# Rings of the split weight tiles four deep instead of two, each tile split by one 1024-column instruction, and a software DMA scratch of 2048 bytes

## The chip, the cores and the metric

The kernel runs on one core of one Trainium2 chip. The metric is the device time of one launch, in microseconds. The engines named below are PE (TensorE, matmuls; PEld is its weight load), ACT (ScalarE), DVE (VectorE), POOL (GpSimd, which here only issues DMAs from the software queue) and SP (SyncE, which issues the DMAs of the hardware queue).

## What is computed

A two-layer trunk on x of 256 tokens by 1024. Each layer has an attention mixer and then a channel mixer with retrieved experts (PEER). The change touches only the second part, which the reference writes so:

```python
def peer(h, w_q, sub_keys, u_tab, v_tab):
    q = jnp.einsum('td,de->te', xt, w_q).reshape(t, PEER_HEADS, 2, PEER_DQ // 2)
    sc = jnp.einsum('thpd,hpnd->thpn', q, sub_keys)          # 8 heads, 2 sides, 128 keys
    # top 16 of each side, top 16 of their 256 sums: eidx (one of 128*128 experts), gates
    ...
    a = jnp.einsum('tkd,td->tk', u_tab[ib], xb)              # u row of each picked expert
    a = jax.nn.gelu(a, approximate=False) * gb
    return jnp.einsum('tk,tkd->td', a, v_tab[ib])            # weighted sum of v rows
for l in range(DEPTH):                                       # DEPTH = 2
    x = x + g1 * mixer(...)
    x = x + g2 * peer(rmsnorm(x, norm_ffn[l]) * (1 + sc2) + sh2, ...)
```

The kernel does not gather. It computes the scores of all 16,384 experts for all tokens (128 tiles of 128 experts), applies a dense table of gates that is zero where an expert was not picked, and multiplies with all of v.

## The kernel before, in words

**Tiles and numbers.** A tile of u or v is 128 partitions by 1024 columns of float32 (512 KB). PE multiplies in one-pass float32r, so each tile is split in two parts: ACT copies it to `hi` (rounded), DVE computes `lo = raw - hi`. Three products (hi with x_hi, hi with x_lo, lo with x_hi) stand for one float32 product.

**The stages of a layer's expert part** (`experts` of each engine):
- *Queries and retrieval*: PE makes the queries and key scores; DVE finds the top 16s, partly beside the first u tiles.
- *Up*: for each of 128 u tiles, PE runs 24 matmuls of 256 columns (`up`), ACT applies gelu to the result (`gelu`), and SP spills it to `s_store` in HBM. Between them stand the matmuls that transpose the picks (`picks`) and build the gate table (`group`).
- *Down*: for each of 128 v tiles, SP fetches the spilled scores into one of four buffers (`back`), DVE multiplies them by the gates (`weigh`), ACT and DVE split the product into a_hi and a_lo (`split_a`, `lower_a`, rings of two), and PE runs 12 matmuls of 512 columns (`down`).

**The rings.** `raw` holds four tiles as loaded. `hi` and `lo` hold two tiles (`SPLITS`), filled and released by halves: `split(n, r, h, ...)` on ACT and `lower(n, r, h)` on DVE work on 512 columns, and the semaphores hi_done, lo_done and w_used count halves.

**What sets the order.** Everything is written out by hand, with one program for each engine, each in strict order. In the down stage, step j is:
- ACT (`down_step`): both halves of split for tile j+2, then `split_a` for tile j+2, which waits until PE has finished tile j.
- DVE (`down_step`): `weigh` for j+2, both halves of lower for j+2, `lower_a` for j+2. In layer 0, every fourth step then reduces one tile of layer 1's modulation weights (`next_modulation`).
- SP (`down_loads`): load v tile j once `lo` of tile j-4 is done, then fetch the scores of tile j+1, which waits for `lower_a` of tile j-3 (al_done). In layer 0, after every fourth tile (j % 4 == 2), it also issues a load of 512 KB of modulation weights (`load_mod1`), ahead of v tile j+1.
- POOL, in layer 0's down stage: seven loads of layer 1's w_in and bias tables into parts of the gate table that are no longer needed, each as soon as `weigh` has come far enough.

In the up stage, step n of ACT is: the first half of split n+2, gelu n, the second half of split n+2. PE's `up(n)` waits for gelu n-2, since two PSUM banks alternate.

Of the kernel before, what the change touches and what calls it, by code (L numbers as in the profile page):

```python
# [8 lines left out]
ALU = mybir.AluOpType  # L9
ACT = mybir.ActivationFunctionType  # L10
F32 = mybir.dt.float32
# [4 lines left out]
P = 128  # L16
# [17 lines left out]
SPLITS = 2  # L34
# [102 lines left out]
def build(nc, a, out):  # L137

    with ExitStack() as ctx:
# [178 lines left out]
        def _(sp):  # L318
# [16 lines left out]
            for l in range(LAYERS):  # L335
# [33 lines left out]
                for n in range(4, 8):  # L369
                    sp.wait_ge(s[l]["lo_done"], 2 * n - 6)  # L370
                    load_u(n, n % 4)
                    if n >= 6:
                        spill(n - 6, n - 6)
                with sp.Fori(2, NKEY // 4) as i:
                    for r in range(4):
                        sp.wait_ge(s[l]["lo_done"], 8 * i + 2 * r - 6)
# [8 lines left out]
                for n in range(NKEY, NKEY + 8):  # L385
                    sp.wait_ge(s[l]["lo_done"], 2 * n - 6)
# [6 lines left out]
                def down_loads(j, i, r, fetches=True):  # L393
                    sp.wait_ge(s[l]["lo_done"], STREAM - 6 + 2 * j)
# [22 lines left out]
                sp.wait_ge(s[l]["lo_done"], 2 * STREAM)  # L417
# [40 lines left out]
        def _(pe):  # L458
# [178 lines left out]
            def experts(l):  # L637

                def up(n, r, wait=True):
# [3 lines left out]
                    o = bank[4 + r][:, 0:T]  # L643
                    for h in range(2):
                        pe.wait_ge(s[l]["hi_done"], 2 * n + h + 1)
                        pe.wait_ge(s[l]["lo_done"], 2 * n + h + 1)
                        for k in range(h * KT // 2, (h + 1) * KT // 2):
                            c = slice(k * P, (k + 1) * P)
                            mm(o, hi[:, r, c], x_hi[:, k, :], k == 0, False)
                            mm(o, hi[:, r, c], x_lo[:, k, :], False, False)  # L650
                            last = mm(o, lo[:, r, c], x_hi[:, k, :], False, k == KT - 1)
                        last.then_inc(s[l]["w_used"], 1)
# [10 lines left out]
                def down(j, r, first=False, end=False):  # L663

                    pe.wait_ge(s[l]["ah_done"], j + 1)
                    pe.wait_ge(s[l]["al_done"], j + 1)
                    for h in range(2):
                        pe.wait_ge(s[l]["hi_done"], STREAM + 2 * j + h + 1)
                        pe.wait_ge(s[l]["lo_done"], STREAM + 2 * j + h + 1)
                        c = slice(h * HALF, (h + 1) * HALF)  # L670
                        for t in range(TT):
                            o, tok = bank[2 * t + h][:, :], slice(t * P, (t + 1) * P)
                            mm(o, a_hi[:, r, tok], hi[:, r, c], first, False, True)
                            mm(o, a_hi[:, r, tok], lo[:, r, c], False, False, True)
                            last = mm(o, a_lo[:, r, tok], hi[:, r, c], False, end, True)
                        last.then_inc(s[l]["w_used"], 1)
# [3 lines left out]
                up(0, 0, False)  # L680
                up(1, 1, False)
# [752 lines left out]
```

## Time and profile before

| | us |
|---|---|
| median of 3 runs (lowest, highest) | 2186.24 (2186.05, 2189.31) |
| the profiled execution, its own time | 2186.42 |
| its span | 2184.6 |
| PE busy, share of the span | 94% |
| PEld | 84% |
| DVE | 67% |
| ACT | 47% |
| DMA queues, hardware / software, share of 16 engines | 57.6% / 6.2% |

The span is the time from the first to the last instruction in the profile; the execution's own time is 1.8 us longer. Busy times are sums over an engine's instructions, and as matmuls are pipelined and their ends modelled, a busy PE is not one at its peak: the distance from one matmul's start to the next tells more. The down stage of layer 0 lies at 764.2 to 1139.4 us, that of layer 1 at 1818.75 to 2167.3 us.

### The profile page before, as it was taken

To read this page: it belongs to the slowest core of one execution; us is meant where nothing else is said; L and a number is where in the kernel's file an instruction comes from. 1 tells how busy PE (TensorE), PEld (TensorE's weight loads), DVE (VectorE), ACT (ScalarE), POOL (GpSimd) and SP (SyncE) were. 2 spreads that over 40 slices of the span, in tenths; PEclk is the share of its full clock that TensorE was granted. 3 is DMA by queue.
4 is the path that set the end of the run, shared out by engine and by line. 5 is a ranking of instruction groups with operands and counts; after the bars stand their busy time and mean duration, and the time that the engine had idled before them with its cause. 6 is when DMAs were issued, how large, how long until landed. Compare 5 with 4: busy or idle time off the path is not lost.

```text
span 2184.6 us, 43826 instructions
## 1 busy us (share of the span) xinstructions
PE 2064.4 (94%) x12608; PEld 1839.8 (84%) x12608; DVE 1463.0 (67%) x3698; ACT 1022.4 (47%) x2012; POOL 18.8 (1%) x39
## 2 busy tenths in 40 slices
PE   2987899999999999999999799999999999999998
PEld 2745799999999977777778478999999998888886
DVE  4463687837777577788771327784877756777776
ACT  2012235635555555555551322563555555555554
POOL 0000000000000000000000000000000000000000
PEclk5998899999999999999999899999999999999999
DMA  9653537736566789998860412774555568777774
GB/s 396 236 187 141 199 111 229 219 108 177 172 176 171 240 292 308 309 318 280 310 216 1 173 41 85 236 221 125 173 176 172 176 194 250 242 241 241 241 241 157
DMA packets 168453, 446.75 MB, mean 204 GB/s; under 512 B 18752, under 2 KB 85568, under 8 KB 163792
## 3 DMA queue, kind: packets, MB, share of 16 engines
q1 hardware_dynamic: 163472, 392.65, 57.6%
q0 software_dynamic: 4928, 53.45, 6.2%
q8 instruction: 27, 0.44, 0.1%
q14 instruction: 26, 0.21, 0.0%
HBM read 409.32 MB, written 36.70 MB: 204 GB/s over the span
## 4 chain that ended last, share of the span: by engine, by line
PE 88%; DMA 5%; DVE 3%; ACT 2%; issue 1%; SPq 0%; DVEq 0%; ACTq 0%
PE bank L460 87%; DMA raw<-in_v 3%; DMA big<-in_w_mod 2%; DMA wmod_ring<-in_w_mod 1%; ACT big L787 1%; DVE big L954 1%; DVE big L1011 1%; PE bank L532 1%; DVE wmod_ring L1320 0%; ACT hi L834 0%; SPq L330 0%; DVE raw L946 0%; DVE a_lo L1194 0%; PE bank L710 0%; DVE big L1043 0%
## 5 line engine op out<-in xcount | busy, mean ns | idle before, releaser
L1175 DVE TENSOR_TENSOR lo<-raw,hi 128x512 fp32r<-128x512 f32 x1024 | 702.9, 691 | 377.8 <-ACT hi L834 372.1
L834 ACT ACTIVATE hi<-raw 128x512 fp32r<-128x512 f32 x1024 | 642.1, 629 | 515.1 <-PE bank L460 477.3
L460 PE MATMUL bank<-x_hi,hi 128*128 128x256 f32 x2048 | 590.2, 288 | 1.6 <-ACT work L840 1.6
L460 PE MATMUL bank<-x_hi,lo 128*128 128x256 f32 x2048 | 579.2, 283 | 0.0
L460 PE MATMUL bank<-x_lo,hi 128*128 128x256 f32 x2048 | 579.1, 283 | 0.0
L460 PE MATMUL bank<-hi,a_hi 128*128 128x512 f32 x1024 | 403.0, 394 | 13.8 <-DVE a_lo L1194 12.4
L460 PE MATMUL bank<-hi,a_lo 128*128 128x512 f32 x1024 | 400.1, 391 | 0.0
L460 PE MATMUL bank<-lo,a_hi 128*128 128x512 f32 x1024 | 399.8, 390 | 0.0
L460 PEld LDWEIGHTS bank<-x_hi,hi 128*128 128x128 f32 x2048 | 392.3, 192 | 1.9 <-issue 1.9
L460 PEld LDWEIGHTS bank<-x_lo,hi 128*128 128x128 f32 x2048 | 392.7, 192 | 0.0
L460 PEld LDWEIGHTS bank<-x_hi,lo 128*128 128x128 f32 x2048 | 392.1, 191 | 0.0
L460 PE MATMUL bank<-raw,big 128*128 128x256 f32 (+1 forms) x1248 | 287.3, 390 | 30.6 <-ACT raw L761 29.1
L460 PEld LDWEIGHTS bank<-raw,big 128*128 128x128 f32 (+1 forms) x1248 | 238.2, 193 | 70.4 <-issue 35.3
L460 PEld LDWEIGHTS bank<-hi,a_hi 128*128 128x128 f32 x1024 | 192.8, 188 | 66.6 <-issue 26.3
L460 PEld LDWEIGHTS bank<-hi,a_lo 128*128 128x128 f32 x1024 | 193.0, 188 | 40.9
L460 PEld LDWEIGHTS bank<-lo,a_hi 128*128 128x128 f32 x1024 | 193.0, 189 | 39.3
L840 ACT ACTIVATE work<-bank 128x256 f32<-128x256 f32 x256 | 98.3, 384 | 195.6 <-PE bank L460 194.9
L1183 DVE TENSOR_SCALAR wmod_ring<-cst,wmod_ring 128x128 f32<-128x128 f32 x512 | 142.4, 342 | 0.0
L460 PE MATMUL bank<-wmod_ring 128*128 128x128 f32 x1024 | 135.1, 275 | 0.0
L460 PEld LDWEIGHTS bank<-wmod_ring 128*128 128x128 f32 x1024 | 125.7, 192 | 0.0
L1189 DVE TENSOR_TENSOR wmod_ring<-wmod_ring,big 128x256 f32<-128x256 f32 x256 | 107.2, 420 | 0.8 <-DMA wmod_ring<-s_store 0.8
L862 ACT ACTIVATE a_hi<-wmod_ring 128x256 fp32r<-128x256 f32 x256 | 103.5, 404 | 8.4 <-DVE wmod_ring L1189 8.3
(142 smaller groups left out, 1313.2 us busy)
## 6 DMA issues: line engine op xcount, KB each, us to landing
raw<-in_u SPq DMA_DIRECT2D x256, 512.0 KB, 4.0
raw<-in_v SPq DMA_DIRECT2D x256, 512.0 KB, 4.5
s_store<-work SPq DMA_DIRECT2D x256, 128.0 KB, 3.7
wmod_ring<-s_store SPq DMA_DIRECT2D x256, 128.0 KB, 3.5
wmod_ring<-in_w_mod SPq DMA_DIRECT2D x54, 512.0 KB, 5.4
big<-in_w_mod SPq DMA_DIRECT2D x40, 512.0 KB, 5.1
big<-in_w_in POOLq DMA_DIRECT2D x10, 2048.0 KB, 11.6
big<-in_w_q POOLq DMA_DIRECT2D x16, 1024.0 KB, 6.5
```

The lines of the kernel that those rows point to most:

```text
L460: return nc.tensor.matmul(o, w, x, start=start, stop=stop, skip_group_check=free)
L532: last = nc.tensor.transpose(bank[4 + n % 2][:, c * P:(c + 1) * P], scores[:, i, c * P:(c + 1) * P], ident)
L787: last = f(c, c, ACT.Exp, bias=neg[:, 2 * i + t:2 * i + t + 1], accum_out=den[:, 2 * i + t:2 * i + t + 1])
L834: f(hi[:, r % 2, c], raw[:, r, c], ACT.Copy).then_inc(s[l]["hi_done"], 1)
L840: f(work[:, r, :], bank[4 + r % 2][:, 0:T], ACT.Gelu).then_inc(s[l]["s_gelu"], 1)
L862: f(a_hi[:, r % 2, :], back[:, b, :], ACT.Copy).then_inc(s[l]["ah_done"], 1)
L954: v.tensor_tensor_reduce(first_mods[r], first_mods[r], c_all[:], 1.0, 0.0, ALU.mult, ALU.add, mod[l][:, n:n + 1]).then_inc(s[l]["mod_tile" ...
L1011: v.tensor_tensor_reduce(scores[:, i, c], bank[i % 4][:, c], b[:, c], 1.0, -3e38, ALU.add, ALU.max, mx[:, 2 * i + t:2 * i + t + 1]).then_i ...
L1175: v.tensor_tensor(lo[:, r % 2, c], raw[:, r, c], hi[:, r % 2, c].bitcast(F32), ALU.subtract).then_inc(s[l]["lo_done"], 1)
L1183: ins = v.tensor_scalar(hot[r % 2][:, 1, n, :], iota, pick[:, 1, bass.ds(4 * g + n, 1)], pick[:, 2, bass.ds(4 * g + n, 1)], ALU.is_equal, ...
L1189: v.tensor_tensor(back[:, b, :], back[:, b, :], gates[:, bass.ds(j, 1), :].rearrange("p a t -> p (a t)"), ALU.mult)\
```

## The change

`SPLITS` is 4, so `hi` and `lo` together take 16 KB more of each partition, and the scratch that is set aside for the descriptors of software DMAs goes from its default down to 2048 bytes of a partition. Split and lower become one instruction of 1024 columns each, and hi_done, lo_done and w_used count tiles. Split of tile n now waits for w_used of tile n-4 and stands one tile further ahead in ACT's and DVE's programs: the up step n does split n+3 and then gelu n; the down step j does split (and lower) for j+3, and then `split_a` (and `lower_a`) for j+2. PE's loops are unrolled by four instead of two, and `up` and `down` wait once for a tile instead of once for a half. What SP issues, in which order, and what each issue waits for is the same but for the counting.

```diff
-SPLITS = 2
+SPLITS = 4
@@ SP
                 def down_loads(j, i, r, fetches=True):
-                    sp.wait_ge(s[l]["lo_done"], STREAM - 6 + 2 * j)
+                    sp.wait_ge(s[l]["lo_done"], NKEY - 3 + j)
                     load_v(j, r)
                     if fetches:
                         fetch(j + 1, (r + 1) % 4, i + (1 if r == 3 else 0))
@@ PE
-                    for h in range(2):
-                        pe.wait_ge(s[l]["hi_done"], 2 * n + h + 1)
-                        pe.wait_ge(s[l]["lo_done"], 2 * n + h + 1)
-                        for k in range(h * KT // 2, (h + 1) * KT // 2):
...
+                    pe.wait_ge(s[l]["hi_done"], n + 1)
+                    pe.wait_ge(s[l]["lo_done"], n + 1)
+                    for k in range(KT):
...
+                    last.then_inc(s[l]["w_used"], 1)
@@ ACT
-                def split(n, r, h, round_, wait=True):
+                def split(n, r, round_, wait=True):
                     act.wait_ge(raw_in[r], 16 * (round_ + 1) + 16 * l * (STREAM // RAWS))
                     if wait:
-                        act.wait_ge(s[l]["w_used"], 2 * n + h - 3)
-                    c = slice(h * HALF, (h + 1) * HALF)
-                    f(hi[:, r % 2, c], raw[:, r, c], ACT.Copy).then_inc(s[l]["hi_done"], 1)
+                        act.wait_ge(s[l]["w_used"], n - 3)
+                    f(hi[:, r], raw[:, r], ACT.Copy).then_inc(s[l]["hi_done"], 1)
...
                 def up_step(n, r, round_, wait=True):
-                    nr, nround = (r + 2) % 4, round_ + (r + 2) // 4
-                    split(n + 2, nr, 0, nround)
+                    split(n + 3, (r + 3) % 4, round_ + (r + 3) // 4, wait or r > 0)
                     gelu(n, r, round_, wait)
-                    split(n + 2, nr, 1, nround)
...
                 copy_keys(PH - 1)
+                split(2, 2, 0, False)
...
-                def down_step(j, r, round_):
-                    nr, nround = (r + 2) % 4, round_ + (r + 2) // 4 + NKEY // 4
-                    for h in range(2):
-                        split(NKEY + 2 + j, nr, h, nround)
-                    split_a(j + 2, r, nr)
+                def down_step(j, a, r, round_):
+                    if j is not None:
+                        split(NKEY + 3 + j, (r + 3) % 4, round_ + (r + 3) // 4 + NKEY // 4)
+                    split_a(a, r, (r + 2) % 4)
@@ DVE
-                def lower(n, r, h):
-                    dve.wait_ge(s[l]["hi_done"], 2 * n + h + 1)
-                    c = slice(h * HALF, (h + 1) * HALF)
-                    v.tensor_tensor(lo[:, r % 2, c], raw[:, r, c], hi[:, r % 2, c].bitcast(F32), ALU.subtract).then_inc(s[l]["lo_done"], 1)
+                def lower(n, r):
+                    dve.wait_ge(s[l]["hi_done"], n + 1)
+                    v.tensor_tensor(lo[:, r], raw[:, r], hi[:, r].bitcast(F32), ALU.subtract).then_inc(s[l]["lo_done"], 1)
...
+                def down_step(j, r, round_, mods=None, left=True):
                     weigh(j + 2, (r + 2) % 4, round_ + (r + 2) // 4)
-                    for half in range(2):
-                        lower(NKEY + 2 + j, (r + 2) % 4, half)
+                    if left:
+                        lower(NKEY + 3 + j, (r + 3) % 4)
                     lower_a(j + 2, r, (r + 2) % 4)
                     if mods:
                         next_modulation(*mods)
@@ host
-    nc = bacc.Bacc("TRN2", target_bir_lowering=False, num_devices=1)
+    nc = bacc.Bacc("TRN2", target_bir_lowering=False, num_devices=1, dynamic_dma_scratch_size=2048)
```

ACT, layer 0's down loop, its first step (j a multiple of four), before. `raw_in2` is the load of tile j+2, w_used_0 the count of what PE has used.

```order
L832 ISA [waits raw_in2]
L834 ACTIVATE hi<-raw 128x512 [waits w_used_0]
L832 REGISTER_ALU [waits raw_in2]
L834 ACTIVATE hi<-raw 128x512 [waits w_used_0]
L859 REGISTER_ALU
L861 ISA [waits a_ready_0]
L862 ACTIVATE a_hi<-wmod_ring 128x256 [waits w_used_0]
```

The same step in the changed kernel.

```order
L834 ISA [waits raw_in3]
L835 ACTIVATE hi<-raw 128x1024 [waits w_used_0]
L858 REGISTER_ALU
L860 REGISTER_ALU [waits a_ready_0]
L861 ACTIVATE a_hi<-wmod_ring 128x256 [waits w_used_0]
```

The split ahead of `a_hi` of tile j+2 is now that of tile j+3, whose load is raw_in3.

DVE, the same step before; s_in2 is the fetch of the scores of tile j+2.

```order
L1189 ISA [waits s_in2]
L1189 TENSOR_TENSOR wmod_ring<-wmod_ring,big 128x256
L1173 ISA
L1175 TENSOR_TENSOR lo<-raw,hi 128x512 [waits hi_done_0]
L1173 REGISTER_ALU
L1175 TENSOR_TENSOR lo<-raw,hi 128x512 [waits hi_done_0]
L1193 REGISTER_ALU
L1194 TENSOR_TENSOR a_lo<-wmod_ring,a_hi 128x256 [waits ah_done_0]
```

And in the changed kernel.

```order
L1186 ISA [waits s_in2]
L1186 TENSOR_TENSOR wmod_ring<-wmod_ring,big 128x256
L1171 REGISTER_ALU
L1172 TENSOR_TENSOR lo<-raw,hi 128x1024 [waits hi_done_0]
L1190 REGISTER_ALU
L1191 TENSOR_TENSOR a_lo<-wmod_ring,a_hi 128x256 [waits ah_done_0]
```

One instruction of 1024 columns, for tile j+3, stands where two of 512 for tile j+2 stood; `a_lo` behind it is still that of tile j+2.

ACT, layer 0, where the up stage begins, before: the copies of `hi` are of tile 2 and then of tile 3, and `work` is gelu of tile 0.

```order
L834 ACTIVATE hi<-raw 128x512 [waits w_used_0,raw_in2]
L840 ACT_TABLE_LOAD
L840 ACTIVATE work<-bank 128x256 [waits w_used_0]
L834 ACTIVATE hi<-raw 128x512 [waits w_used_0,raw_in2]
L834 ACTIVATE hi<-raw 128x512 [waits w_used_0,raw_in3]
```

And in the changed kernel.

```order
L835 ACTIVATE hi<-raw 128x1024 [waits raw_in2]
L835 ACTIVATE hi<-raw 128x1024 [waits raw_in3]
L841 ACT_TABLE_LOAD
L841 ACTIVATE work<-bank 128x256 [waits w_used_0]
```

Two whole tiles are split ahead of the first gelu, where half of one was.

## Rows read from the trace of the kernel before

**Rows 1.** Stretches of both down stages: us; busy by engine; PEclk, DMA share, GB/s.

```profile
764.20:1139.40 375.20, 361.18 (x1538) 287.58 (x1536) 295.44 (x607) 201.65 (x382) 3.71 (x7) 0.99 0.88 296
1818.75:2167.30 348.55, 348.35 (x1538) 288.11 (x1536) 260.06 (x508) 199.54 (x382) 0.00 (x0) 1.00 0.76 237
```

**Rows 2.** Waits of PE in layer 0's down stage: us, times, longest.

```profile
PE bank L460 <- DVE a_lo L1194: 12.4, 6, 3.6
```

**Rows 3.** Chain of waits: start us, us, what; first and last of a kind.

```profile
778.03 11.16 PE bank L460 x48
...
1108.54 11.17 PE bank L460 x48
```

**Rows 4.** Timeline of layer 0's down stage around one modulation load: start us, us.

```profile
828.11 0.39 PE L460 MATMUL bank<-hi,a_hi 128*128 128x512 f32 x1
828.31 0.63 ACT L834 ACTIVATE hi<-raw 128x512 fp32r<-128x512 f32 x1 [0.73 <-PE bank L460]
828.85 0.40 ACT L862 ACTIVATE a_hi<-wmod_ring 128x256 fp32r<-128x256 f32 x1
...
829.58 0.42 DVE L1194 TENSOR_TENSOR a_lo<-wmod_ring,a_hi 128x256 fp32r<-128x256 f32 x1
...
830.18 0.33 SPq L350 DMA_DIRECT2D wmod_ring<-s_store  x1
...
830.78 0.33 SPq L333 DMA_DIRECT2D wmod_ring<-in_w_mod  x1
...
831.41 0.33 SPq L340 DMA_DIRECT2D raw<-in_v  x1
...
832.64 1.22 DVE L1199 CUSTOM_DVE_ANT_0 wmod_ring<-wmod_ring,c_all 128x1024 f32<-128x1024 f32 x1
...
835.69 0.42 DVE L1194 TENSOR_TENSOR a_lo<-wmod_ring,a_hi 128x256 fp32r<-128x256 f32 x1
...
836.47 0.47 PE L460 MATMUL bank<-hi,a_hi 128*128 128x512 f32 x1
...
838.25 0.63 ACT L834 ACTIVATE hi<-raw 128x512 fp32r<-128x512 f32 x1 [0.84 <-DMA raw<-in_v]
```

**Rows 5.** Landing of raw's loads at 864:898, 975:1037, 1830:2160, 480:740, in order.

```profile
DMA to landing us min/median/max: 4.2/4.7/6.2
DMA to landing us min/median/max: 3.9/5.0/6.7
DMA to landing us min/median/max: 3.5/4.3/5.2
DMA to landing us min/median/max: 3.7/3.8/4.2
```

**Rows 6.** Chain of waits through v loads issued beside POOL's loads.

```profile
802.91 11.00 DMA raw<-in_v
...
816.35 0.34 issue
...
1038.54 12.59 DMA raw<-in_v
```

**Rows 7.** Busy time by stretch, just after PE's stall at 861.9 to 863.9.

```profile
863.90:867.30 3.40, 3.40 (x8) 2.66 (x9) 1.90 (x4) 2.07 (x4) 0.00 (x0) 0.53 1.03 375
```

**Rows 8.** Groups by form: busy us, mean ns, idle before.

```profile
L1175 DVE TENSOR_TENSOR lo<-raw,hi 128x512 fp32r<-128x512 f32 x1024 | 702.9, 691 | 377.8 <-ACT hi L834 372.1
L1325 DVE TENSOR_TENSOR x_lo<-raw,x_hi 128x2048 fp32r<-128x2048 f32 x2 | 4.6, 2293 | 5.1 <-ACT x_hi L827 5.1
L822 ACT ACTIVATE big<-raw 128x1024 f32<-128x1024 f32 x1 | 1.1, 1057 | 1.5 <-DVE raw L1051 1.5
```

**Rows 9.** Timeline where layer 0's up stage begins.

```profile
309.55 0.36 PE L460 MATMUL bank<-x_hi,hi 128*128 128x256 f32 x1
311.74 0.63 ACT L834 ACTIVATE hi<-raw 128x512 fp32r<-128x512 f32 x1 [1.32 <-DMA raw<-in_u]
312.39 1.28 ACT L840 ACT_TABLE_LOAD   x1
```

More of the change, by code:

```diff
@@ L672, in down @@
                             o, tok = bank[2 * t + h][:, :], slice(t * P, (t + 1) * P)
[L673 to L676, printed above, removed]
+                            mm(o, a_hi[:, r % 2, tok], hi[:, r, c], first, False, True)
+                            mm(o, a_hi[:, r % 2, tok], lo[:, r, c], False, False, True)
+                            last = mm(o, a_lo[:, r % 2, tok], hi[:, r, c], False, end, True)
+                    last.then_inc(s[l]["w_used"], 1)
                 pe.wait_ge(s[l]["xh_done"], 1)
                 pe.wait_ge(s[l]["xl_done"], 1)
-                up(0, 0, False)
-                up(1, 1, False)
-                with pe.Fori(1, GROUP_AT // 2 - 1) as i:
-                    for r in range(2):
-                        up(2 * i + r, r)
+                for r in range(4):
+                    up(r, r, r >= 2)
+                with pe.Fori(1, GROUP_AT // 4 - 1) as i:
+                    for r in range(4):
+                        up(4 * i + r, r)
+                for r in range(2):
+                    up(GROUP_AT - 4 + r, r)
                 picks(l)
-                for r in range(2):
-                    up(GROUP_AT - 2 + r, r)
+                for r in range(2, 4):
+                    up(GROUP_AT - 4 + r, r)
                 for r in range(4):
-                    up(GROUP_AT + r, r % 2)
+                    up(GROUP_AT + r, r)
                     group(r, r, False)
@@ L692, in experts @@
                     for r in range(4):
[L693 removed]
+                        up(GROUP_AT + 4 * i + r, r)
                         group(4 * i + r, r)
[L695 to L697 removed]
+                with pe.Fori((GROUP_AT + GROUPS) // 4, NKEY // 4) as i:
+                    for r in range(4):
+                        up(4 * i + r, r)
                 pe.wait_ge(s[l]["g_copied"], GROUPS)
                 down(0, 0, first=True)
[L700 to L703 removed]
+                with pe.Fori(0, NKEY // 4 - 1) as i:
+                    for r in range(4):
+                        down(4 * i + 1 + r, (1 + r) % 4)
+                for r in range(1, 4):
+                    down(NKEY - 4 + r, r, end=r == 3)
             def expert_out(l):
@@ L1219, in experts @@
                         for n in range(2):
-                            for half in range(2):
-                                lower(n, n, half)
+                            lower(n, n)
                 for n in range(GROUP_AT - 2):
-                    for half in range(2):
-                        lower(n + 2, (n + 2) % 4, half)
-                        advance(500)
+                    lower(n + 2, (n + 2) % 4)
+                    advance(1000)
                 for _ in left:
@@ L1232, in experts @@
                 for g in range(4):
-                    for half in range(2):
-                        lower(GROUP_AT + g, g, half)
+                    lower(GROUP_AT + g, g)
                     one_hot(g, g, g >= 2)
@@ L1237, in experts @@
                     for r in range(4):
-                        for half in range(2):
-                            lower(GROUP_AT + 4 * i + r, r, half)
+                        lower(GROUP_AT + 4 * i + r, r)
                         one_hot(4 * i + r, r)
@@ L1242, in experts @@
                     for r in range(4):
-                        for half in range(2):
-                            lower(4 * i + r, r, half)
+                        lower(4 * i + r, r)
                 dve.wait_ge(s[l]["g_copied"], GROUPS)
```

55 lines of the change are left out of this document (22 added, 33 removed).

## The prediction

> **What bounds the kernel now.** I read the busy time by stretch first. Layer 1's down stage shows a clean PE: 128 tiles in 348.55 us, 2.72 us a tile, PE busy all the time [rows 1]. Layer 0's, with the same 128 tiles, takes 375.20 us, 26.65 us more [rows 1]. The list of PE's waits and the starts of its matmuls in both layers' up stages show next to nothing, so these 26.65 us are nearly all that a deeper ring could give back, and they are the place where it can also lose. Three things fill them.
>
> First, PE's chain runs there in pieces of 48 matmuls, four tiles, of 11.16 or 11.17 us [rows 3], against 4 x 2.72 = 10.89. Each piece ends in a gap of about 0.28 us; I count 27 such gaps among the starts, from 778.03 to 1119.74 us: 27 x 0.28 = 7.6 us. The timeline around one of them shows why. DVE spends 1.22 us on the modulation weights at 832.64; a_lo of the next tile then starts at 835.69 and ends at 836.11, and PE starts at 836.47 instead of at about 836.27 [rows 4]. Second, PE waits for a_lo six times, 12.4 us in all, up to 3.6 [rows 2]. Here v loads landed late: the load issued at 802.91 took 11.00 us, the one at 1038.54 took 12.59 [rows 6], because a software DMA of 2 or 3 MB ran at that moment (POOL issues seven such loads there, five of them large). Third, the clock: after the stall that ended at 863.90 the granted clock was 0.53 for 3.4 us, 1.2 instead of 2.4 GHz, and eight matmuls ran in the time of four [rows 7], 1.6 us lost. After one other stall it was the same. 7.6 + 12.4 + 3.2 leaves 3.4 us for restarts and a slightly slower pace.
>
> **The time line of a v tile.** All of the rest hangs on this. Call the tile Y and count from the moment t = 0 at which PE starts tile Y-5 (828.11 in the rows). ACT sees the end of Y-6 at 0.20; `a_hi` of Y-4 takes 0.40; a_lo takes 0.42; the fetch is issued 0.18 after a_lo's end, and v tile Y 0.61 after the fetch, or 1.23 after it where a modulation load stands between [rows 4]. In the kernel before, half a split stands ahead of a_hi and a lower ahead of a_lo, so a_lo ends at 1.89 and the load of Y goes out at 3.30 behind a modulation load [rows 4].
>
> The order matters more than the depth. The fetch of Y still waits for a_lo of Y-4, and SP issues v tile Y only behind it. So the load of Y can't leave before PE is done with Y-6, however many slots `hi` has. Now without the half split, a_lo ends at 0.20 + 0.40 + 0.03 + 0.42 = 1.05 and the load goes out at 1.84, or at 2.46 behind a modulation load: 0.8 us earlier.
>
> But it is needed a whole tile earlier. In step j of ACT and DVE, split and lower of j+3 stand ahead of split_a and lower_a of j+2. A late Y therefore holds back a_hi and a_lo of Y-1, which PE needs after four tiles, at 10.89, where before it held back only its own a_lo, needed at 13.61. And the way from landing to PE is longer with whole tiles: 0.12 hand-over (a load issued at 831.41 lets ACT start at 838.25, and its landing is at most 6.7 [rows 4, 5]), 1.09 for a split of 1024 columns (1.06 for another 1024-column copy [rows 8]), 0.03, 1.15 for lower (between 0.69 at 512 and 2.29 at 2048 columns it is 1.23; the next starts 0.08 before its end [rows 8]), a_lo 0.42, and 0.34 until PE runs [rows 6]: 3.15 us. Load times that pass without a stall: before, 13.61 - 2.42 - 2.65 = 8.5 us; now 10.89 - 1.84 - 3.15 = 5.9, and 5.3 behind a modulation load.
>
> **The change part by part.**
> - *Gaps behind the modulation work.* In the new order a_lo of step j ends at 1.05, then 1.5 of modulation work, 0.34 weigh, 1.2 lower, 0.42 lower_a: done at 4.6 + 0.34, needed at 5.44. The gaps go: -7.6. At worst they stay (0).
> - *Loads behind a modulation load.* The largest landing times in quiet parts of this stage are 6.2 and 6.7, the medians 4.7 and 5.0 [rows 5]; in the timeline the load behind the modulation load is the one for which ACT waits 0.84 us [rows 4]. Taken as 6.4, the middle of 6.2 and 6.7, it gives 2.46 + 6.4 + 3.15 - 10.89 = 1.1 us of stall for the first. For those after it there is a feedback: DVE does lower_a late, then weigh and a whole lower, before lower_a of Y-4, which ends at 1.57 instead of 1.05. So the load leaves at 2.98 and the stall is 1.65. I take 1.4, between both. There are 30 modulation loads in this stage, 5 beside large POOL loads (next item): 25 x 1.4 = 35.0. Bounds: 0, if the load lands in under 5.3 us; 25 x 1.94 = 48.5 with 6.7 and the later issue.
> - *The five large POOL loads.* Landing 11.0 four times and 12.6 once [rows 6] gives L - 5.9 = 5.1 x 4 + 6.7 = 27.1 us of stall, against 12.4 now [rows 2]: +14.7. Such stalls are longer than the one after which the clock fell, so I add 1.6 us for the three that are spared now [rows 7]: +4.8. Bounds: 0 and 25.
> - *Layer 1's down stage.* No modulation, no POOL loads. Landing at most 5.2 [rows 5] < 5.9: 0. If single loads pass 5.9, some tenths each: at most +3.
> - *Up stages.* A late u tile now also holds back a gelu, but u lands in at most 4.2 [rows 5], and between its issue and the gelu's need lie over 8 us. The ACT work per tile falls a little and is not on the path: 0, bounds -1 to +2. Only the start differs: tile 2's split can start at 311.74 as now, then tile 3's (its load lands about 313.0), 1.1, then 1.28 of table load and 0.38 of gelu, where half a split stood before. PE could start tile 2 at 309.55 + 2 x 2.88 = 315.3 [rows 9] and will at about 316.1: 0.85 in each layer, +1.7.
> - *PE waiting once a tile, loops unrolled by four, fewer semaphore steps.* PE has a matmul start every 0.120 us in the up stage with or without a half's boundary: 0, bounds -2 to +2.
> - *Scratch of 2048 bytes.* No row shows what a smaller ring of descriptors does. From below: if it slows POOL's loads so that they press less on v, it gives back up to the 19.5 us of the item above. From above: if one of the layer's first loads from POOL comes late by a large one's 11 us on the path: +11. POOL's issues are far apart and their landings hidden under other stages, so I take 0.
>
> The Trainium skill's page "SBUF — State Buffer", section "SBUF size: 192, 224, or 256?", says that this scratch is 16 KiB and is the ring for software-made descriptors; no run here shows a price for it.
>
> **Sum.** -7.6 + 35.0 + 14.7 + 4.8 + 1.7 = +48.6 us on the profiled execution's 2186.4: 2235.0. Its time is within 0.2 us of the median of the runs, so 2235 us stands for a run as well.
>
> **A rule against the trace.** The rows show a load in this stage landing 3.9 to 6.7 us after its issue [rows 5]. The page "DMA: Bandwidth & Descriptors" of the Trainium skill, section "Anatomy of one DMA — SWDGE (gpsimd) path", fits a transfer by 2.0 us + bytes / 436e3. By it the fetch, the modulation load and the v load, 1.18 MB in a row, are in after an estimated 4.7 us, under the 5.3 that pass, and the sum without the 35.0 would hold. The trace has a duration for the same thing, so the sum uses that; rival 2 is what the rule would make of it.
>
> **Rivals.**
> 1. *Faster: the depth does bring slack.* If loads land early enough, or if the earlier issue (0.8 us) spreads them so that the late ones vanish, the stalls stay as they are and only the gaps go: 2186.4 - 7.6 + 1.7 = 2180.5. It decides where the landing behind a modulation load is under 5.3 us and those beside POOL's loads under about 8.5. For it: the issue is earlier and PE's own demand is the same. Against it: the DMA engines are busy 0.88 of this stage [rows 1], and 6.7 and 11.0 are far from the limits.
> 2. *Only POOL's loads count.* Modulation loads cause nothing: 2186.4 - 7.6 + 14.7 + 4.8 + 1.7 = 2200.0. For it: the margin in question, 1.1 us, is small beside 6.4.
> 3. *Heavier.* The loads stand closer (2.5 us between v tiles Y-1 and Y instead of 3.3), so that landing goes to 6.7 or over and stalls feed on each other: 48.5 instead of 35.0, 2248.5, and more with longer landings.
> 4. *The deeper ring does nothing*, since the fetch's wait holds the loads where they are: gaps gone, stalls smaller than reckoned, within 4 us of 2186.
>
> **How the numbers follow.** Forecast 0.60, with its own range 2216 to 2252; rival 1 0.12; rival 2 0.16; rival 3 0.08; rival 4 0.04. What a measurement here can tell from no change is 0.2%, 4.4 us. Faster 0.12 (rival 1), same 0.04, slower 0.84. The range holds the forecast and rival 2 with the lower part of rival 3, and leaves out rivals 1 and 4: 2193 to 2255.
>
> **What would show it.** In the new profile, layer 0's down stage takes about 420 us, layer 1's 348 to 349. PE waits for a_lo about 30 times: about 25 waits of 1 to 2 us, each behind a modulation load, and five of 5 to 7. ACT's 1024-column copy waits there for the DMA of in_v, and behind each late one comes a_hi and a_lo of the tile before it. The gaps of 0.28 are gone. The up stages have the same length but for one wait for gelu 0. I am wrong if layer 0's down stage is under 375 us (then landing is shorter than the rows say, or the order of split and split_a costs nothing), or if layer 1's is over 352.

## The result, and the profile after

The kernel after takes 2226.74 us, median of 4 runs (2220.14 to 2231.97), against 2187.27 (2186.05 to 2189.31) for the kernel before in the same job: ratio 1.0178, 95% interval 1.0148 to 1.0208. It is slower, and 8 us under the 2235 forecast. The profiled execution of after took 2224.59 us with a span of 2222.8, that of before 2186.42 with 2184.6.

Both down stages of after by stretch (length, busy time by engine, PE's granted clock, DMA share, GB/s), answering to [rows 1]; the third line is 3.4 us just behind one of the long stalls, answering to [rows 7]:

```profile
768.51:1177.75 409.24, 365.45 (x1538) 292.92 (x1536) 280.85 (x478) 179.03 (x253) 3.69 (x7) 0.97 0.79 271
1856.91:2205.26 348.35, 348.35 (x1538) 288.24 (x1536) 249.52 (x379) 184.81 (x253) 0.00 (x0) 1.00 0.76 237
819.67:823.07 3.40, 3.40 (x9) 2.68 (x9) 1.64 (x3) 2.42 (x3) 0.00 (x0) 0.53 0.86 303
```

Layer 1's down stage is the matmuls alone: 348.35 us, PE never idle. I call this the pace. Layer 0's, with the same matmuls, takes 409.24 us; before, from first to last matmul, it took 374.98. That is 34.3 of the 38.2 us by which the span grew. PE's waits for a_lo there, answering to [rows 2] (us, times, longest), and in a second fence ACT's waits for v tiles in the same stage:

```profile
PE bank L460 <- DVE a_lo L1191: 42.6, 25, 5.9
```

```profile
ACT hi L835 <- DMA raw<-in_v: 133.0, 80, 7.9
```

The starts of the matmuls, read from the timeline, tell the two kinds apart: 22 stalls of 0.6 to 1.7 us, 25.8 us over the pace, and five of 3.4 to 6.1 us, 22.1 us. A stall of the first kind, answering to [rows 4] (start us, us, engine and line; other rows of the stretch left out):

```profile
825.77 0.33 SPq L333 DMA_DIRECT2D wmod_ring<-in_w_mod  x1
826.36 0.33 SPq L340 DMA_DIRECT2D raw<-in_v  x1
...
832.80 1.06 ACT L835 ACTIVATE hi<-raw 128x1024 fp32r<-128x1024 f32 x1 [2.65 <-DMA raw<-in_v]
...
833.77 0.40 ACT L861 ACTIVATE a_hi<-wmod_ring 128x256 fp32r<-128x256 f32 x1
833.89 1.23 DVE L1172 TENSOR_TENSOR lo<-raw,hi 128x1024 fp32r<-128x1024 f32 x1 [2.46 <-ACT hi L835]
...
835.04 0.42 DVE L1191 TENSOR_TENSOR a_lo<-wmod_ring,a_hi 128x256 fp32r<-128x256 f32 x1
...
835.80 0.47 PE L460 MATMUL bank<-hi,a_hi 128*128 128x512 f32 x1 [0.78 <-DVE a_lo L1191]
```

The v load goes out behind a modulation load and lands 6.3 us later. ACT has stood idle for 2.65 us. Its split and DVE's lower belong to tile Y; the `a_hi` and `a_lo` behind them belong to tile Y-1, and it is these for which PE waits. From landing to PE it is 3.1 us. The same in the chain of waits beside a software load (start us, us, what), answering to [rows 6]:

```profile
808.39 8.26 DMA raw<-in_v
816.67 1.06 ACT hi L835
...
818.90 0.43 DVE a_lo L1191
819.33 0.34 issue
819.67 4.48 PE bank L460 x12
```

### The profile page after: what moved, and what is told of

The parts are those of the page before. It is cut to its first block, busy times and chain, and to the rows that moved or that the text cites. A ratio compares the mean times of both kernels' runs of the same rounds, so it can differ in the third digit from the quotient of the medians.

```text
span 2222.8 us, 40544 instructions
## 1 busy us (share of the span) xinstructions
PE 2073.0 (93%) x12608; PEld 1849.0 (83%) x12608; DVE 1414.8 (64%) x3186; ACT 939.9 (42%) x1500; POOL 18.7 (1%) x39
## 4 chain that ended last, share of the span: by engine, by line
PE 75%; DMA 12%; DVE 5%; ACT 3%; issue 3%; SPq 1%; DVEq 0%; ACTq 0%
PE bank L460 74%; DMA raw<-in_v 9%; DMA big<-in_w_mod 2%; ACT hi L835 1%; DVE a_lo L1191 1%; DMA wmod_ring<-in_w_mod 1%; ACT big L789 1%; DVE lo L1172 1%; DVE big L952 1%; DVE big L1009 1%; PE bank L532 1%; SPq L350 1%; SPq L333 0%; DMA raw<-in_u 0%; DVE wmod_ring L1312 0%
## 5 line engine op out<-in xcount | busy, mean ns | idle before, releaser
L1172 DVE TENSOR_TENSOR lo<-raw,hi 128x1024 fp32r<-128x1024 f32 x512 | 625.4, 1222 | 280.7 <-ACT hi L835 279.6
L835 ACT ACTIVATE hi<-raw 128x1024 fp32r<-128x1024 f32 x512 | 540.2, 1055 | 186.2 <-DMA raw<-in_v 179.2
L1177 DVE TENSOR_TENSOR wmod_ring<-cst,wmod_ring 128x512 f32<-128x512 f32 x128 | 88.7, 693 | 115.0 <-PE bank L460 115.0
L1191 DVE TENSOR_TENSOR a_lo<-wmod_ring,a_hi 128x256 fp32r<-128x256 f32 x256 | 108.1, 422 | 50.2 <-ACT a_hi L861 47.0
```

The costliest lines, as they stand in the source:

```text
L835: f(hi[:, r], raw[:, r], ACT.Copy).then_inc(s[l]["hi_done"], 1)
L1172: v.tensor_tensor(lo[:, r], raw[:, r], hi[:, r].bitcast(F32), ALU.subtract).then_inc(s[l]["lo_done"], 1)
L1177: v.tensor_tensor(hot[r % 2][:, 0], iota.unsqueeze(1).to_broadcast([P, 4, P]), pick[:, 0, bass.ds(4 * g, 4)].unsqueeze(2).to_broadcast([P, ...
L1191: v.tensor_tensor(a_lo[:, r % 2, :], back[:, b, :], a_hi[:, r % 2, :].bitcast(F32), ALU.subtract).then_inc(s[l]["al_done"], 1)
```

## The experiments

All times are medians, with the ratio to the kernel before timed on the same chip. Two numbers describe each: layer 0's down stage from first to last matmul, and what of it lies over the pace of 348.35. Layer 1's down stage is 348.35 wherever nothing else is said. Medians of different kernels are to be compared with care, for a reason shown at the end: one wait ahead of the experts is some 8.5 us shorter in some executions, in kernels with the old rings and with the new.

### 1. The order turned round, on ACT and DVE

```diff
-                        split(NKEY + 3 + j, ...)
-                    split_a(a, r, (r + 2) % 4)
+                    split_a(a, r, (r + 2) % 4)
+                        split(NKEY + 3 + j, ...)
...
-                        lower(NKEY + 3 + j, (r + 3) % 4)
-                    lower_a(j + 2, r, (r + 2) % 4)
+                    lower_a(j + 2, r, (r + 2) % 4)
+                        lower(NKEY + 3 + j, (r + 3) % 4)
```

> The kernel after, with only the order inside a step of the expert down stage turned round on ScalarE and VectorE: split_a/lower_a of tile j+2 ahead of split/lower of tile j+3. Theory (order): in the kernel after a late load of tile Y holds back a_hi and a_lo of tile Y-1, so it is late 2.7 us earlier than its own data would be; with the order turned only tile Y's own halves wait. Then the 22 stalls of 0.6 to 1.7 us behind a modulation load (25.8 us in all) go, the five of 3.4 to 6.1 us beside GpSimd's loads lose 2.7 us each (22.1 to about 9), layer 0's down stage falls from 409.2 to about 370 to 375 us and the time from 2226.7 to 2186 to 2192 us. Rival A (landing): the weight tiles just land later, whatever the order: the stage stays 405 to 412, the time 2222 to 2230. Rival B (width: whole 1024-column instructions and one wait for a whole tile add 0.5 us between landing and matmul): only the larger part of the order goes, stage 385 to 395, time 2203 to 2213.

Measured: 2304.43 us, ratio 1.0539 (1.0511 to 1.0568). All three expectations missed. Layer 0's down stage is 447.01 us, and layer 1's, which no theory had touched, 390.76:

```profile
1893.36:2284.12 390.76, 380.65 (x1538) 278.61 (x1536) 250.65 (x379) 171.93 (x253) 0.00 (x0) 1.00 0.68 211
```

The timeline of one tile there (start us, us) shows why. ACT waits 1.71 us for weigh (L1186), not for data:

```profile
2000.23 0.42 DVE L1186 TENSOR_TENSOR wmod_ring<-wmod_ring,big 128x256 f32<-128x256 f32 x1
...
2000.76 0.42 ACT L861 ACTIVATE a_hi<-wmod_ring 128x256 fp32r<-128x256 f32 x1 [1.71 <-DVE wmod_ring L1186]
...
2001.09 1.04 ACT L835 ACTIVATE hi<-raw 128x1024 fp32r<-128x1024 f32 x1
...
2002.16 1.23 DVE L1172 TENSOR_TENSOR lo<-raw,hi 128x1024 fp32r<-128x1024 f32 x1 [0.52 <-ACT hi L835]
...
2003.30 0.42 DVE L1186 TENSOR_TENSOR wmod_ring<-wmod_ring,big 128x256 f32<-128x256 f32 x1
```

weigh, split_a, split, lower, and weigh again: each waits for the one before, two by semaphore and two by the order of their engine. The ring takes 3.07 us a turn, and 390.76 / 128 = 3.05 us a tile is what the stage runs at, against 2.72 of the matmuls. So this run says nothing on whether the order costs in the kernel after. It shows that an order can close a ring between two engines that is slower than the engine they feed.

### 2. The weight load one tile earlier on SP

```diff
                     load_v(j, r)
-                    if fetches:
-                        fetch(j + 1, (r + 1) % 4, i + (1 if r == 3 else 0))
+                    fetch(j, r, i)
```

> The kernel after, with only SyncE's order changed: the weight load of tile j stands ahead of the load of the gelu tile j, not of j+1, so it no longer waits for a_lo of tile j-4 but of tile j-5 and leaves one tile (2.72 us) earlier. Theory (order, with SyncE's wait for a_lo as the gate): the stalls up to 1.7 us behind a modulation load all go (25.8 us), the five large ones lose 2.7 us each (22.1 to about 9): layer 0's down stage 368 to 375 us, time 2186 to 2193. Rival A (landing: the transfers are bound by the DMA engines at 0.88 of their time, an earlier issue only waits in the queue): stage 400 to 412, time 2218 to 2230. Rival B (width): as in the run before, 385 to 395 and 2203 to 2213.

Measured: 2188.59 us, ratio 1.0012 (0.9994 to 1.0031). Stage 380.51, 32.2 over the pace. The small stalls are gone, all 22; the five large ones are not (21.6 us by the matmul starts):

```profile
PE bank L459 <- DVE a_lo L1190: 20.9, 5, 5.7
```

```profile
807.76 12.13 DMA raw<-in_v
```

The first half of the theory held, the second failed. The load does leave a tile earlier, but now in the same moment as a modulation load (807.17) and a software load of 2 MB (807.14), and it takes 12.1 us instead of 8.3. It lands at 819.9; in after, the load issued at 808.39 landed at 816.7.

### 3. Both edits of 1 and 2

(The two diffs above together.)

> Both edits together: split_a/lower_a ahead of split/lower, and the weight load one tile earlier on SyncE. Theory (order): a weight tile then has about 5.9 + 2.7 + 2.7 = 11.3 us to land against 8.5 in the kernel before, so of the 12.4 us of waits beside GpSimd's loads there nearly all goes too, and so do the 0.28 us gaps of the kernel before (7.6 us): layer 0's down stage 356 to 362 us (bound of the matmuls alone about 355), time 2168 to 2180, faster than both kernels. Rival A (landing): stage above 400, time 2218 to 2230. Rival C (the DMA engines are full while GpSimd loads, so the stalls there stay at 12 us however early the weights are asked for): stage 368 to 372, time 2181 to 2187.

Measured: 2296.94 us, ratio 1.0512 (1.0485 to 1.0538); down stages 438.50 and 390.78. The ring of experiment 1 again. The loads are not late here (PE's longest wait for a_lo is 1.7 us), and it doesn't matter.

### 4. The scratch alone, on the kernel before

```diff
-    nc = bacc.Bacc("TRN2", target_bir_lowering=False, num_devices=1)
+    nc = bacc.Bacc("TRN2", target_bir_lowering=False, num_devices=1, dynamic_dma_scratch_size=2048)
```

> The kernel before with the software DMA scratch of 2048 bytes alone. Theory: nothing, 2185 to 2190 us, GpSimd's loads land in the same time and the stalls beside them stay 12.4 us. Rival D (the smaller scratch slows or staggers GpSimd's loads, and part of the 9.7 us by which the large stalls grew is its doing): 2190 to 2200 us, or GpSimd's loads land more than 10% later.

Measured: 2185.19 us, ratio 1.0004 (0.9987 to 1.0022), stage 375.69. GpSimd's loads of 2 MB land in a median of 11.1 us (11.6 before). The scratch is worth nothing, as forecast.

### 5. The order turned round without the ring

```diff
-                    weigh(j + 2, (r + 2) % 4, round_ + (r + 2) // 4)
+                    lower_a(j + 2, r, (r + 2) % 4)
                     if left:
+                        weigh(j + 3, (r + 3) % 4, round_ + (r + 3) // 4)
                         lower(NKEY + 3 + j, (r + 3) % 4)
-                    lower_a(j + 2, r, (r + 2) % 4)
```

(ACT as in experiment 1; one weigh more ahead of the loop.)

> The order turned round once more (split_a/lower_a of tile j+2 ahead of split/lower of tile j+3), but now with weigh of tile j+3 in front of lower of tile j+3 on VectorE. Revised theory: the swap alone lost because it closed a ring of waits in every tile: weigh 0.3, split_a 0.43, split 1.07, lower 1.23 and again weigh, with four hand-overs some 3.05 us (390.8 us for 128 tiles in layer 1's down stage, which nothing else loads) against the 2.72 us of the matmuls. With weigh ahead the ring is open: layer 1's down stage is 348 to 349 us again, and a weight tile in layer 0 has 5.9 + 2.7 = 8.6 us to land: all small stalls go, the five large ones shrink, stage 374 to 382 us, time 2182 to 2190. Rival (the order is not what costs in the kernel after; the swap lost through something else, like ScalarE's wait for a_ready): layer 1's down stage stays above 370, or layer 0's above 400.

Measured: 2182.54 us, ratio 0.9977 (0.9959 to 0.9995).

```profile
767.22:1136.98 369.76, 357.77 (x1538) 293.45 (x1536) 285.93 (x477) 174.57 (x253) 3.69 (x7) 0.98 0.87 300
1818.06:2166.41 348.35, 348.34 (x1538) 288.11 (x1536) 250.21 (x378) 172.28 (x253) 0.00 (x0) 1.00 0.76 237
```

```profile
PE bank L460 <- DVE a_lo L1191: 12.0, 5, 4.2
```

Layer 1 is at the pace again, which confirms the ring. In layer 0 all small stalls are gone and the five large ones are nearly halved, to 12.8 us by the matmul starts: 369.76 is 39.5 us less than in after, by the order of a few instructions. This is the run that shows that the order is what makes after slow. Not all of it is the order alone: behind a modulation load the v load also leaves earlier here, 2.4 us after PE's start of tile Y-5 against 2.8 in after (medians). And experiment 2 took away the same small stalls with the order left as it was. So it takes both, a load that lands late and an order that makes the tile before it wait. It is also what the change could have given: a little under the kernel before, whose gaps of 0.28 us are gone too.

### 6. The transfers one by one

From the kernel after, the modulation loads of the stage cut to 8 columns, which leaves out most of layer 1's modulation weights:

```diff
-                                load_mod1(2 * i + r // 4 + MIXED_MODS, r // 4)
+                                load_mod1(2 * i + r // 4 + MIXED_MODS, r // 4, 8)
```

> The kernel after with the 27 modulation loads of layer 0's down stage but the first two cut from 1024 to 8 columns (this leaves out most of layer 1's modulation weights; everything else is as it was). Theory (queue): 22 small stalls (25.8 us) go, and the five large ones beside GpSimd's loads lose the part of a modulation load that lands with them, about 1.2 us each: stage 409.2 to 377 to 384 us, time 2194 to 2202. Rival (the small stalls come from the order or the wide instructions and only happen to stand at every fourth tile, where VectorE does 1.7 us of modulation work): they stay, stage 400 to 409, time 2217 to 2227.

Measured: 2202.49 us, ratio 1.0066 (1.0042 to 1.0090), stage 387.46, 39.1 over the pace. Two stalls of 0.5 us and two of 0.3 to 0.4 are left of the small ones, so they are the modulation loads' and not the modulation work's, which DVE still does. The large ones did not shrink (25.0 us; expected some 16): the wrong part of the expectation, by which the stage was to be 377 to 384. The run shows why. The v loads beside the five large software loads leave 1.9 to 2.3 us after PE's start of tile Y-5, where in after they leave 3.7 to 4.5 after it, but they land 10.8, 10.5, 9.7, 10.8 and 11.9 us later, where in after it takes 8.3 to 10.9. What is gained at the issue is lost in the landing.

And the software loads cut to 8 columns, which leaves out most of layer 1's input weights and bias tables:

```diff
+                    e = b + 8 if l else e
                     pool.dma_start(big[:, b:e], w[:, b:e]).then_inc(win_in[n], 16)
...
+                nb = 8 if l else nb
```

> The kernel after with GpSimd's seven loads for layer 1 in the down stage cut to 8 columns each (this leaves out layer 1's input weights and bias maps; everything else is as it was). Theory: the five stalls of 3.4 to 6.1 us (22.1 us) go with the slower matmuls behind them (about 2 us), the stalls of 1 to 1.7 us behind modulation loads stay, and about three to five more of them show where the large ones hid them: stage 409.2 to 386 to 391 us, time 2203 to 2209. Rival (the small stalls too come from a stage that GpSimd's loads keep behind): most small ones go as well, stage 355 to 370, time 2172 to 2188.

Measured: 2201.98 us, ratio 1.0067 (1.0045 to 1.0089), stage 391.56, 43.2 over the pace, just above what was expected.

```profile
PE bank L462 <- DVE a_lo L1193: 33.9, 28, 2.0
```

```profile
767.79:1159.35 391.56, 356.24 (x1538) 285.82 (x1536) 279.62 (x478) 180.09 (x253) 3.77 (x7) 1.00 0.76 251
```

The large stalls are gone and the clock is 1.00, but now each of the 30 modulation loads makes a small one: 30 stalls, 40.1 us, 1.34 each, where after has 22 with 25.8. The large stalls had covered eight and shortened others, so taking them away gives 17.7 us and not the 32 that they and their clock cost. The DMA share is 0.76 here, the same as in layer 1, and the stage still loses 43 us: a short queue behind one transfer is enough.

### 7. The halves again

```diff
-                    f(hi[:, r], raw[:, r], ACT.Copy).then_inc(s[l]["hi_done"], 1)
+                    for h in range(2):
+                        c = slice(h * HALF, (h + 1) * HALF)
+                        f(hi[:, r, c], raw[:, r, c], ACT.Copy).then_inc(s[l]["hi_done"], 1)
```

(lower likewise, one half beside the next split.)

> The kernel after with each 1024-column split and lower cut into two of 512 columns again, the second half of the one beside the first of the other; the rings stay four deep, the order stays that of after, TensorE still waits for whole tiles. Theory (order first, width second): landing to matmul falls by about 0.5 us (3.15 to 2.65), so each of the 22 small and five large stalls loses 0.5 us: layer 0's down stage 409.2 to 393 to 399 us, time 2211 to 2217. Rival (width is what costs): the stage falls below 385. Rival (width is nothing, or 512-column instructions cost as much as they give): 405 to 412.

Measured: 2213.97 us, ratio 1.0116 (1.0086 to 1.0147), but stage 406.07, only 3.2 us under after. By the stage, which the edit acts on, it is the rival "width is nothing": 19 small stalls with 25.0 us, four large with 18.3. I had the sum wrong: from the start of ACT's split to the start of a_lo behind a late tile it is 1.87 us here and 2.24 in after (timelines at 1052.70 and 832.80), 0.37 less and not 0.5. Over 27 stalls even that would be 10 us. The stage gives back 3.2, since the v loads land later here (median over 775 to 1095 us 5.2 us, against 4.9 in after); why they do is open. The medians differ by 13 us, the profiled spans (2219.7 and 2222.8) by 3 like the stage; the other 10 are within what the part ahead of the experts varies by.

### 8. The bursts cut up

On the kernel of experiment 2, GpSimd's loads for layer 1 in pieces of 512 KB:

```diff
-                    if l:
-                        pool.wait_ge(s[0]["a_ready"], -(-e // T))
-                    pool.dma_start(big[:, b:e], w[:, b:e]).then_inc(win_in[n], 16)
+                    for b in range(b, e, D if l else e - b):
+                        d = min(b + D, e) if l else e
+                        if l:
+                            pool.wait_ge(s[0]["a_ready"], -(-d // T))
+                        pool.dma_start(big[:, b:d], w[:, b:d]).then_inc(win_in[n], 16)
```

> The kernel with the weight load one tile earlier on SyncE (the last but two run), and GpSimd's loads for layer 1 in the down stage cut into pieces of 1024 columns (512 KB), each issued when its own gate columns are free. Theory (burst): the 20.9 us of waits left there are 2 MB bursts that the weight tiles queue behind (landing 12.1 us against 4 to 5); a piece of 512 KB every four tiles delays a tile by about as much as a modulation load does, 1 to 2 us, which 8 us of room hide: layer 0's down stage 355 to 362 us, time 2162 to 2172, faster than both kernels. Rival (bytes): the DMA engines are at 0.88 of their time over the stage, so the same bytes cost the same whether in bursts or not: stage 372 to 381, time 2180 to 2189. Rival (software DMA): 25 small transfers cost more on GpSimd's queue than 7 large ones: above 381.

Measured: 2172.11 us, ratio 0.9921 (0.9892 to 0.9951), stage 356.10, as the burst theory had it. The same bytes and a higher DMA share (0.88 against 0.84 in experiment 2), and 24 us less. What is left are eight waits of up to 1.0 us. A piece and a modulation load start in the same moment there, every four tiles:

```profile
816.56 0.53 POOL L440 DMA_DIRECT2D big<-in_w_in  x1 [10.43 <-DVE wmod_ring L1189]
```

```profile
816.52 0.33 SPq L333 DMA_DIRECT2D wmod_ring<-in_w_mod  x1
```

So each piece was put two tiles later:

```diff
-                            pool.wait_ge(s[0]["a_ready"], -(-d // T))
+                            pool.wait_ge(s[0]["a_ready"], -(-d // T) + 2)
```

> The pieces kernel (weight load one tile earlier, GpSimd's loads in pieces) with each piece two tiles later, so that it no longer starts in the same moment as a modulation load (816.56 against 816.52 us there). Theory (what counts is what lands together): the waits of up to 1.0 us (6.5 us in all) go: layer 0's down stage 356.1 to 350 to 353 us, time 2164 to 2169. Rival (the DMA engines at 0.90 of their time are the limit, the phase is nothing): 355 to 357, time 2170 to 2174.

Measured: 2163.06 us, ratio 0.9892 (0.9868 to 0.9915).

```profile
758.11:1106.46 348.35, 348.35 (x1538) 288.21 (x1536) 286.68 (x478) 175.58 (x253) 12.67 (x24) 1.00 0.91 316
```

The stage is at the pace of the matmuls, with a DMA share of 0.91 and not one wait for a_lo: better than expected. Median landing over 775 to 1095 us (KB each, us) went from 6.1 to 5.2 for v tiles and from 7.2 to 5.1 for the pieces:

```profile
raw<-in_v SPq DMA_DIRECT2D x115, 512.0 KB, 6.1
...
big<-in_w_in POOLq DMA_DIRECT2D x17, 512.0 KB, 7.2
```

```profile
raw<-in_v SPq DMA_DIRECT2D x116, 512.0 KB, 5.2
...
big<-in_w_in POOLq DMA_DIRECT2D x17, 512.0 KB, 5.1
```

The first fence is of the pieces, the second of the shifted pieces.

### 9. Everything, and the pieces on the kernel before

The edits of experiments 2 and 5 and the unshifted pieces together:

> All three edits on the kernel after: the turned order with weigh ahead, the weight load one tile earlier on SyncE, GpSimd's loads in pieces of 512 KB. Theory (room to land): a weight tile has about 11 us against landings of 5 to 8.6, so the 6.5 us of waits of the pieces run go, and its stage of 356.1 us falls to 348.5 to 351, the pace of the matmuls alone (348.35 in layer 1): time 2162 to 2168. Rival (the matmuls' own limit or the clock is all that is left at 356): stage 354 to 358, time 2169 to 2175. Rival (turned order: a closed ring of waits again under the earlier loads): layer 1's down stage above 360 us.

Measured: 2162.40 us, ratio 0.9877 (0.9850 to 0.9904); down stages 348.34 and 348.35. This reaches the pace too, although pieces and modulation loads coincide as in the first kernel of experiment 8 (over 775 to 1095 us v tiles land in up to 8.5 us): here there is room for it. It is the fastest of all by its ratio, level with the shifted pieces.

And the pieces alone on the kernel before:

> The kernel before with GpSimd's loads for layer 1 in the down stage cut into pieces of 512 KB, nothing else. Theory (burst): the 12.4 us of waits beside them and the 1.7 us of slow clock go, the 27 gaps of 0.28 us stay: layer 0's down stage 375.0 to 359 to 364 us, time 2172 to 2178; so most of what the best kernel gains is this edit's and not the deeper rings'. Rival (before's rings, two tiles deep, have no room to spare for a piece and a modulation load that land together): waits of 1 us at every fourth tile, stage 370 to 380.

Measured: 2163.51 us, ratio 0.9905 (0.9880 to 0.9930).

```profile
757.94:1116.32 358.38, 356.99 (x1538) 285.73 (x1536) 295.89 (x606) 202.71 (x381) 12.67 (x24) 1.00 0.89 310
```

The waits for a_lo are gone, and 10.0 us over the pace are left, of which the gaps of 0.28 us, 30 here, are 8.4. So of the 26.6 us that layer 0's down stage lost before, 16.6 were the bursts and can be had without any deeper ring; the deep rings in a better order add the last 10. That is read from the stages. The medians would mislead twice. This one lies 24.5 us under that of the kernel before, and 8 to 14 under what was expected, because in the profiled execution the part ahead of the experts was 6.2 us shorter too. And it lies only 1.1 us over the kernel with all edits, whose profiled execution had the longer start.

## Why the prediction was right, term by term

The order of events was as forecast, and the sign follows from it. The sizes of layer 0's down stage, over the pace:

| term | forecast | measured |
|---|---|---|
| 0.28 us gaps | 7.6 to 0 | 7.6 to 0 |
| behind modulation loads | 25 x 1.4 = 35.0 | 22 x 1.17 = 25.8 |
| beside the five large software loads | 12.4 to 27.1: +14.7 | 13.4 to 22.1: +8.7 (matmul starts) |
| clock (in the measured column with restarts) | +4.8 | 5.6 to 13.0: +7.4 |
| sum | +46.9 | +34.3 |

- **The time line.** A v load lands 6.3 us after its issue where 6.4 was assumed, and from landing to PE it is 3.1 where 3.15 was. The late tile holds back the tile before it, as the first timeline shows. Experiment 5 takes this away and the stage falls by 39.5 us.
- **Behind modulation loads.** This term was mis-sized by its count and by its neighbours. The 1.4 us a stall is close for a stage in which nothing else stalls (1.34 in 30, experiment 6). In after a large stall lets the loads catch up, so eight of the 30 modulation loads cost nothing and others cost less. I had taken out only the five that stand beside a large load.
- **Beside the software loads.** Two errors that partly cancel. The working took landings of 11.0 four times and 12.6 over from before; by the chain of waits they are 8.3, 9.1, 8.9, 9.1 and 10.9 in after, 10.4 us less in all. And it gave each load 5.9 us that pass without a stall; landing less stall is 4.7 to 4.9 in all five, since a small stall just before sends the load out later, a feedback that I had counted for the modulation loads only: 5.4 us more in all. So the five are 22.1 and not 27.1 us. The run without modulation loads (experiment 6) bears out both. With the small stalls gone, landing less stall is 5.6 to 6.0 in all five, the 5.9 of the working, and the landings are 9.7 to 11.9 us, near those of before. By what way the modulation loads and the small stalls shorten the landings in after is not shown.
- **The clock.** This term was mis-sized too. In the 3.4 us after each of the five large stalls the granted clock was 0.50 to 0.57, 1.2 instead of 2.4 GHz. By the matmul starts it was low for 3.1 us after three of them, but for 5.1 and 6.4 after the stalls that ended at 872.62 and 990.77, as the line below shows for the latter, 3.4 us on. The slow matmuls cost 9.8 us in all, against 3.2 before: +6.6, forecast +4.8. The other 0.8 us are restarts and the pace around them.

```profile
994.17:997.57 3.40, 3.40 (x10) 2.63 (x10) 1.49 (x3) 1.31 (x2) 0.53 (x1) 0.59 0.75 249
```

- **Layer 1, up stages, start.** Layer 1's down stage is the same to 0.01 us. The up stages grew by 0.3 and 0.5 us where 0.85 each was forecast, and the part between layer 0's down stage and layer 1's up stage shrank by 0.9. The part ahead of layer 0's up stage grew by 4.0 us, forecast 0. I take this for chance, which is not shown: it ends at 303.3 to 317.3 us in the profiled executions of these kernels, in which nothing is changed there but how the first tiles are split, and the same part in layer 1 takes 224 to 226 us in all of them. By the spans 38.2 us came of the 48.6 forecast, and 4.0 of these are the start's; without it the forecast would have been 4 us further off.
- **Scratch.** Nothing, shown by experiment 4.
- **A room that does not add up.** The working gives a v tile 8.5 us to land in the kernel before. By its own terms the load leaves at 1.89 + 0.18 + 0.61 = 2.68 us, not 2.42, so it would be 8.3, and 7.7 behind a modulation load. The sum does not use this number.
- **Rivals.** Rival 1 (faster, since loads land early enough) is what the fit on the Trainium skill's page "DMA: Bandwidth & Descriptors", section "Anatomy of one DMA — SWDGE (gpsimd) path", would have made of it: 4.7 us, estimated, for what took 6.3. Rival 2 (only the software loads count) falls with experiment 6: without them the stage still lost 43 us. Rival 3 (heavier, by landings of 6.7 us and over) did not come: on the chain of waits the landings not beside a large load had a median of 6.3 (4.9 to 7.2), and the time stayed under the forecast. Rival 4 (nothing happens) falls with the result.
- **What the prediction did not see.** Its list of what DVE and ACT wait for treated the order as a given and priced only what a late load does in it. That another order on the same rings would be worse by 78 us or better by 44 stood nowhere, nor that the loads' bursts, untouched by the change, were worth 16.6 us.

The Trainium skill's page "DMA: Bandwidth & Descriptors", section "Queues, rings and completion order", says that a DMA engine takes turns between the queues that have work for it, packet by packet. The traces fit this but do not show the turns themselves: beside a software load of 2 MB a v tile of 512 KB needs 8.3 to 12.1 us (after and experiment 2) instead of a median of 4.9 to 5.2, and in the stage with pieces of 512 KB it is at most 8.7.

## What to carry to other kernels

A deeper ring gives slack only to what waits for it alone. Before deepening one, follow a late transfer through each in-order engine and ask whose work stands behind it and when that is needed; here the slack of one tile was paid with the tile before it. Whoever reorders must also add up the closed rings of waits between engines, since a ring longer than a step of the bottleneck sets the pace even with no transfer late. And a mean DMA share of 0.9 is no verdict: cut bursts to the size of the tiles beside them and put them where no other load starts, before anything else is rebuilt.

## What was unexpected of the hardware

- **Share and waits are nearly unrelated.** Layer 0's down stage lost 43.2 us at a DMA share of 0.76 (experiment 6), 26.6 at 0.88 (before), and none at 0.91 (shifted pieces).
- **One wait at the start of the program has two lengths.** PE's longest wait there, for `raw` at the first norm, is 16.9 to 17.5 us in three of the 14 profiled executions (scratch alone, pieces on the kernel before, shifted pieces) and 24.2 to 26.2 in the eleven others, from the same code. The three reach the first matmul of the up stage at 303.3 to 307.2 us, the others at 309.6 to 317.3. What decides it is open. Of the six times of the kernel with all edits two are 2153.4 and 2153.6 and four 2162.1 to 2163.5. Here is that wait (us in total, times, longest) in the shifted pieces, then in the kernel with all edits:

```profile
PE bank L463 <- ACT raw L766: 20.5, 4, 16.9
```

```profile
PE bank L463 <- ACT raw L766: 29.0, 4, 25.4
```

- **Which stall lowers the clock isn't told by its length alone.** After a stall of 2.0 us that ended at 818.24 in experiment 5 the clock was 0.55 for 3.4 us; after one of 2.2 us that ended at 895.94 in the kernel without software loads, and after the one of 2.2 us that ended at 816.69 in before, it stayed 1.00. Why is open. The first of the two fences is of experiment 5, the second of the kernel without software loads:

```profile
818.24:821.64 3.40, 3.40 (x9) 2.71 (x10) 1.66 (x3) 2.42 (x3) 0.00 (x0) 0.55 1.01 360
```

```profile
895.94:899.34 3.40, 3.40 (x15) 2.83 (x16) 2.93 (x4) 1.75 (x3) 0.00 (x0) 1.00 0.63 187
```
